# Second branch of the mixer: sums and products on half tiles, products with states ahead of the inner ones, four state buffers

## The reference

```python
def hgrn2_chunked(q, k, v, log_f):
    cum = jnp.cumsum(log_f, axis=-2)
    q_in = q * jnp.exp(cum)
    k_in = k * jnp.exp(-cum)
    intra = jnp.where(causal, jnp.einsum('bhnid,bhnjd->bhnij', q_in, k_in), 0.0)
    last = cum[..., -1:, :]
    k_dec = k * jnp.exp(last - cum)
    chunk_decay = jnp.exp(last[..., 0, :])

    def step(state, xs):
        qi, ki, vi, ai, di = xs
        o = jnp.einsum('bhcd,bhde->bhce', qi, state) + jnp.einsum('bhij,bhje->bhie', ai, vi)
        state = di[..., :, None] * state + jnp.einsum('bhcd,bhce->bhde', ki, vi)
        return state, o
```

## Time and profile before

| | us |
|---|---|
| timed runs, median of 3 | 2370.7 |
| lowest and highest of them | 2370.43 and 2371.64 |
| span of the profiled execution | 2370.3 |
| stretch of the inner matrices, until the loop starts | 7.4 |
| stretch of the loop over the four tiles | 39.6 |

### The profile page before, as it was taken

One profiled execution on the slowest core, in us unless ns is written; L12 is line 12 of the kernel. 1 busy time (PEld: TensorE's weight loads), 2 busy tenths in 40 slices (PEclk: granted clock), 3 DMA queues, 4 the chain that ended last, 5 costly groups with the idle time before them and its releaser, 6 DMA issues. The chain is left out here.

```text
span 2370.3 us, 29415 instructions
## 1 busy us (share of the span) xinstructions
PE 2262.8 (95%) x11234; PEld 1794.2 (76%) x11234; DVE 1506.0 (64%) x1871; ACT 1269.6 (54%) x1680; POOL 276.4 (12%) x273
## 2 busy tenths in 40 slices
PE   7999999999999999999999999999995999999994
PEld 6878558777777768998888878888774777777773
DVE  3534842569978677656334555355337899988886
ACT  4334541588874436552324423235424888888884
POOL 2000000123320212330000000000001111121210
PEclk9999999999999999999999999999996999999997
DMA  6222103423214433001222212334125999999995
GB/s 232 72 71 89 36 21 112 131 76 100 97 61 139 155 125 125 2 1 54 89 95 94 96 36 81 124 115 160 54 101 227 376 408 409 409 402 401 400 401 193
DMA packets 119817, 377.41 MB, mean 159 GB/s; under 512 B 9608, under 2 KB 38592, under 8 KB 94496
## 3 DMA queue, kind: packets, MB, share of 16 engines
q1 hardware_dynamic: 106432, 332.49, 38.0%
q0 software_dynamic: 12768, 37.13, 4.7%
q10 hardware_dynamic: 512, 6.34, 0.6%
HBM read 363.02 MB, written 21.02 MB: 162 GB/s over the span
## 5 line engine op out<-in xcount | busy, mean ns | idle before, releaser
L2270 DVE TENSOR_TENSOR w_lo<-raw,w_hi 128x2048 fp32r<-128x2048 f32 x117 | 267.9, 2290 | 460.0 <-ACT w_hi L1618 459.7
L1618 ACT ACTIVATE w_hi<-raw 128x2048 fp32r<-128x2048 f32 x117 | 223.8, 1913 | 407.5 <-PE bank L863 368.6
L863 PE MATMUL bank<-hT_hi,w_hi 128*128 128x512 f32 x512 | 201.6, 394 | 4.6 <-DVE hT_lo L2334 2.3
L863 PE MATMUL bank<-hT_hi,w_lo 128*128 128x512 f32 x512 | 200.6, 392 | 0.0
L863 PE MATMUL bank<-hT_lo,w_hi 128*128 128x512 f32 x512 | 200.5, 392 | 0.0
L1072 PE MATMUL bank<-hT_hi,w_hi 128*128 128x512 f32 x432 | 173.8, 402 | 0.9 <-DVE hT_lo L2334 0.9
L1072 PE MATMUL bank<-hT_hi,w_lo 128*128 128x512 f32 x432 | 168.2, 389 | 0.0
L1072 PE MATMUL bank<-hT_lo,w_hi 128*128 128x512 f32 x432 | 168.1, 389 | 0.0
L3106 DVE TENSOR_TENSOR e_lo<-eraw,e_hi 128x2048 fp32r<-128x2048 f32 x62 | 141.9, 2290 | 36.1 <-ACT e_hi L2150 36.0
L2990 DVE TENSOR_TENSOR e_lo<-raw,e_hi 128x2048 fp32r<-128x2048 f32 x64 | 146.6, 2291 | 8.2 <-ACT e_hi L2133 7.9
L2990 DVE TENSOR_TENSOR w_lo<-raw,w_hi 128x2048 fp32r<-128x2048 f32 x64 | 144.2, 2286 | 8.9 <-ACT w_hi L2133 8.8
(11 more groups left out here) (590 smaller groups left out, 5344.0 us busy)
## 6 DMA issues: line engine op xcount, KB each, us to landing
raw<-expert_w_gate SPq DMA_DIRECT2D x64, 1024.0 KB, 11.1
raw<-expert_w_up SPq DMA_DIRECT2D x64, 1024.0 KB, 11.6
eraw<-expert_w_down SPq DMA_DIRECT2D x64, 1024.0 KB, 10.8
raw<-w_in SPq DMA_DIRECT2D x40, 1024.0 KB, 5.1
raw<-even_w_in SPq DMA_DIRECT2D x18, 1024.0 KB, 5.3
raw<-odd_w_in SPq DMA_DIRECT2D x16, 1024.0 KB, 5.4
raw<-even_w_out SPq DMA_DIRECT2D x8, 1024.0 KB, 5.1
raw<-odd_w_out SPq DMA_DIRECT2D x8, 1024.0 KB, 5.1
```

What stands on the lines that cost most here:

```text
L863: mm = pe.matmul(out, st, mv, start=first and x == 0, stop=last and x == 2)
L1618: act.activation(split_to(m)[0][:], raw[n % RAW][:], ACT.Copy).then_inc(sem("hi_done"), 1)
L2270: dve.tensor_tensor(split_to(m)[1][:], raw[split_of[m] % RAW][:], f32(split_to(m)[0][:]), ALU.subtract).then_inc(sem("lo_done"), 1)
```

## The change

The inner matrices are made for the two halves apart: for every head and tile two products of a 128 x 64 stationary operand with 64 moving columns, one into partitions 0 to 63 and one into 64 to 127, both into the same 64 columns of the bank. The masked result `hwithin` has 64 columns for each head and tile in place of 128, and the mask is stored accordingly.

The chunk sums of a tile go through the two groups of four heads, and in each head the half s = 0 is followed at once by s = 1. For the last tile only s = 0 is summed. The products with states stand together for the eight heads (`from_states`), and behind them all inner products (`from_chunks`), each of these now two products of 64 rows and 64 columns. The state ahead of the first chunk, which is zero, is neither cleared nor multiplied; the first state is a copy of the first sum. There are four state buffers, and a new semaphore `hs_read` tells DVE that PE has read the states of a tile. The last state isn't formed. The barrier of PE behind the loop is replaced with waits for the last state and for the last output copied.

```diff
+HF = P // 2
+UP, LOW = slice(0, HF), slice(HF, P)
+HALVES = (UP, LOW)
+    in_half = lambda m: m[:, :HF] | m[:, HF:]
-        (i <= j) & same(QC),
+        np.concatenate([in_half((i <= j) & same(QC))] * 2, 1),
+    hwithin = view("hwithin", 0, [P, NT, HEADS, HF], at=8192)
-    hstate = [view(f"hstate{b}", 5, [P, HEADS, P], at=4096 * b) for b in range(3)]
+    hstate = [view(f"hstate{b}", 5, [P, HEADS, P], at=4096 * b) for b in range(4)]
...
             for t in range(NT):
-                ts = slice(t * P, t * P + P)
-                mm = pe.matmul(psum[h][:, ts], hexp[:, h, ts], hqT[:, h, ts], start=True, stop=True)
+                for r in HALVES:
+                    ts = slice(t * P + r.start, t * P + r.stop)
+                    mm = pe.matmul(psum[h][r, t * HF:t * HF + HF], hexp[:, h, ts], hqT[:, h, ts], start=True, stop=True)
...
+        def chunk_sums(t):
+            chunks = range(2 if t < NT - 1 else 1)
+            for hg in range(2):
+                if t:
+                    pe.wait_ge(*after("hs_S", HEADS * (2 * t - 1) + 4 * hg + 4))
+                else:
+                    pe.wait_ge(*after("h_mask", 2 + hg + 1))
+                for h in range(4 * hg, 4 * hg + 4):
+                    for s in chunks:
+                        mm = pe.matmul(psum[2 * s + hg][:, (h % 4) * P:(h % 4) * P + P], hkd[HALVES[s], h, t],
+                                       hv[HALVES[s], t, h * P:h * P + P], start=True, stop=True)
+                        if h % 4 == 3:
+                            mm.then_inc(sem("hs_kv"), 1)
+        def out_bank(t, h):
+            return psum[4 + 2 * (t % 2) + h // 4], slice((h % 4) * P, (h % 4) * P + P)
+        def from_states(t):
+            for h in range(HEADS):
+                bk, cs = out_bank(t, h)
+                if h % 4 == 0 and t >= 2:
+                    pe.wait_ge(*after("hs_o", 2 * (t - 2) + h // 4 + 1))
                 pe.wait_ge(*after("hs_S", HEADS * 2 * t + h + 1))
+                for s, r in enumerate(HALVES):
+                    if t or s:
+                        mm = pe.matmul(bk[r, cs], hqT[:, h, t * P + s * QC:t * P + s * QC + QC], hstate[(2 * t + s) % 4][:, h],
+                                       start=h % 4 == 0, stop=False, skip_group_check=True)
+            mm.then_inc(sem("hs_read"), 1)
+        def from_chunks(t):
+            for h in range(HEADS):
+                bk, cs = out_bank(t, h)
+                for s, r in enumerate(HALVES):
+                    mm = pe.matmul(bk[r, cs], hwithin[r, t, h], hv[r, t, h * P:h * P + P], start=t == 0 and s == 0 and h % 4 == 0,
+                                   stop=True, skip_group_check=True)
+                if h % 4 == 3:
+                    mm.then_inc(sem("hs_ope"), 1)
-        stage()
+        chunk_sums(0)
+        pe.wait_ge(*after("h_mask", HEADS))
+        for t in range(NT):
+            from_states(t)
+            from_chunks(t)
+            if t < NT - 1:
+                chunk_sums(t + 1)
+        stage(wait=False)
+        pe.wait_ge(*after("hs_S", HEADS * (2 * NT - 1)))
+        pe.wait_ge(*after("hs_o", 2 * NT))
 ...
-            dve.tensor_tensor(hintra[:, :, h], psum[h][:].rearrange("p (t j) -> p t j", j=P),
-                              m_hgrn.unsqueeze(1).to_broadcast([P, NT, P]), ALU.mult).then_inc(sem("h_mask"), 1)
+            dve.tensor_tensor(hwithin[:, :, h], psum[h][:, 0:NT * HF].rearrange("p (t j) -> p t j", j=HF),
+                              m_hgrn[:, 0:HF].unsqueeze(1).to_broadcast([P, NT, HF]), ALU.mult).then_inc(sem("h_mask"), 1)
-        own.link(dve.memset(hstate[0][:], 0.0))
-            for s in range(2):
+            for s in range(2 if t < NT - 1 else 1):
-                s_in, s_out = hstate[n % 3], hstate[(n + 1) % 3]
+                s_in, s_out = hstate[n % 4], hstate[(n + 1) % 4]
-                        dve.wait_ge(*after("hs_kv", 2 * n + h // 4 + 1))
+                        dve.wait_ge(*after("hs_kv", 4 * t + (2 if t < NT - 1 else 1) * (h // 4) + s + 1))
-                        if n >= 2:
-                            dve.wait_ge(*after("hs_ope", 2 * ((n - 2) // 2) + 2))
+                        if n >= 3:
+                            dve.wait_ge(sem("hs_read"), (n - 3) // 2 + 1)
+                    if n:
+                        dve.scalar_tensor_tensor(s_out[:, h], s_in[:, h], col(DEC8 + 8 * h + n), kv, ALU.mult, ALU.add).then_inc(sem("hs_S"), 1)
+                    else:
+                        dve.tensor_copy(s_out[:, h], kv).then_inc(sem("hs_S"), 1)
```

More of the change, by code:

```diff
@@ L1376, in _ @@
                 pe.wait_ge(*after("hs_S", HEADS * 2 * t + h + 1))
-                for s in range(2):
-                    r = slice(s * QC, s * QC + QC)
-                    pe.matmul(bk[r, cs], hqT[:, h, t * P + s * QC:t * P + s * QC + QC], hstate[(2 * t + s) % 3][:, h],
-                              start=True, stop=False, skip_group_check=True)
-                mm = pe.matmul(bk[:, cs], hintra[:, t, h], hv[:, t, h * P:h * P + P], start=False, stop=True,
-                               skip_group_check=True)
+                for s, r in enumerate(HALVES):
[9 more added lines that the diff above has]
+                                   stop=True, skip_group_check=True)
                 if h % 4 == 3:
                     mm.then_inc(sem("hs_ope"), 1)
-        stage()
+        chunk_sums(0)
[8 more added lines that the diff above has]
+        pe.wait_ge(*after("hs_o", 2 * NT))
         gemm(pn["og_b"], hT, False)
@@ L2922, in _ @@
             dve.wait_ge(*after("h_in", h + 1))
-            dve.tensor_tensor(hintra[:, :, h], psum[h][:].rearrange("p (t j) -> p t j", j=P),
-                              m_hgrn.unsqueeze(1).to_broadcast([P, NT, P]), ALU.mult).then_inc(sem("h_mask"), 1)
+            dve.tensor_tensor(hwithin[:, :, h], psum[h][:, 0:NT * HF].rearrange("p (t j) -> p t j", j=HF),
+                              m_hgrn[:, 0:HF].unsqueeze(1).to_broadcast([P, NT, HF]), ALU.mult).then_inc(sem("h_mask"), 1)
         stage()
-        own.link(dve.memset(hstate[0][:], 0.0))
         for t in range(NT):
-            for s in range(2):
+            for s in range(2 if t < NT - 1 else 1):
                 n = 2 * t + s
-                s_in, s_out = hstate[n % 3], hstate[(n + 1) % 3]
+                s_in, s_out = hstate[n % 4], hstate[(n + 1) % 4]
                 for h in H8:
                     if h % 4 == 0:
-                        dve.wait_ge(*after("hs_kv", 2 * n + h // 4 + 1))
+                        dve.wait_ge(*after("hs_kv", 4 * t + (2 if t < NT - 1 else 1) * (h // 4) + s + 1))
                         if n:
                             dve.wait_ge(*after("hs_S", HEADS * n))
-                        if n >= 2:
-                            dve.wait_ge(*after("hs_ope", 2 * ((n - 2) // 2) + 2))
+                        if n >= 3:
+                            dve.wait_ge(sem("hs_read"), (n - 3) // 2 + 1)
                     kv = psum[2 * s + h // 4][:, (h % 4) * P:(h % 4) * P + P]
-                    dve.scalar_tensor_tensor(s_out[:, h], s_in[:, h], col(DEC8 + 8 * h + n), kv, ALU.mult, ALU.add).then_inc(sem("hs_S"), 1)
+                    if n:
+                        dve.scalar_tensor_tensor(s_out[:, h], s_in[:, h], col(DEC8 + 8 * h + n), kv, ALU.mult, ALU.add).then_inc(sem("hs_S"), 1)
+                    else:
+                        dve.tensor_copy(s_out[:, h], kv).then_inc(sem("hs_S"), 1)
         stage()
```

16 lines of the change are left out of this document (removed).

## The result

| | us |
|---|---|
| changed kernel, median of 4 | 2349.75 (2349.20 to 2355.68) |
| kernel before, beside it, median of 4 | 2370.56 (2370.35 to 2371.64) |
| ratio | 0.9915, 95% interval 0.9903 to 0.9927 |
| span of the profiled execution | 2347.7; its own time 2349.93 |

The kernel is faster by 20.8 us, or 0.85%.

What follows compares the result with a forecast made beforehand. PE was taken as the bound; loop -15.4, inner matrices -1.7 and loop end -0.2 summed to -17.3 us, span 2353.0, forecast 2353.4 us. The 8-in-10 range was 2350.5 to 2361; the forecast's own, 2350.5 to 2356.5.

Steps and rivals of the forecast that it cites:

- What bounds the kernel: Whole kernel and changed stretch: PE sets the pace ahead of, in and behind the change, so the gain carries through.
- Sums, states, inner products: Loop tile: 16 side-by-side steps per group, 1.79, 1.71 and 1.71 us, plus 0.54 for three shape changes; 5.75 us.
- The 0.1 us a tile added for DVE: Loop: DVE's state updates and PE's arrival nearly level, so each tile was allowed 0.1 us more, 5.85.
- The inner matrices: Ahead of the loop: 128 half-size records take 5.6 us with the shape change, against 7.2; -1.7 us, ends 0 and -3.6.
- the lower bound: Inner matrices: halves fully side by side, 64 steps of 0.053 us, 3.4 us, or 3.6 with the shape change.
- the middle between two ends: Inner matrices: 5.4 us taken between 6.8 one after another and 3.4 side by side, doubting PE's record start rate.
- The end: Behind the loop: PE waits for ACT's last copy, no longer for its 0.19 us mark; -0.2 us.
- The cleared state: Loop start: dropping the first state's clearing and copies gains nothing, as the sums of s = 1 hide them.
- Fourth buffer and last state: Loop: fourth state buffer and `hs_read` cost nothing; the states dropped at the end were included in the loop's -15.4 us.
- The inner products don't run side by side: Rival, loop: halves writing one bank go one after another, 6.8 us more, 2360.2 us; chance 0.20.
- No pair lasts: Rival, loop and inner matrices: side-by-side pairs occur only in bursts; no change, 2371.3 us; chance 0.07.
- The clock falls: Rival, stretch: granted clock drops to 1.2 GHz, steps double, gemm behind loses about 2 us; 2378.8 us; chance 0.05.

Runs made afterwards that it cites:

- experiment 8: Changed kernel with 84 needless 512-column products put ahead of the first products with states, restoring the old timing behind them: 2372.02 us, ratio 1.0005.
- experiment 10: Changed kernel with the output gate's gemm begun early and the chunk sums also cut by key columns into 64 x 64 quadrants: 2353.53 us, stretch 29.82.
- Experiment 9: Changed kernel with the output gate's gemm started on its first two banks before the last two output copies: 2351.86 us, stretch 0.81 us less.
- experiment 2: Kernel before with only the chunk sums reordered, both halves of a head following each other: 2365.78 us, stretch 5.14 us less.
- experiment 6: Changed kernel with the cleared first state and its products put back: 2350.36 us, stretch 0.56 us more.
- experiment 3: Kernel before with only the states' products of all heads placed ahead of the inner products, still 128 wide: 2361.08 us, stretch 9.68 us less.
- experiment 1: Kernel before, unedited, timed and profiled again: 2371.44 us, ratio 1.0001.
- experiment 4: Kernel before with only the inner matrices and their products cut into 64-wide halves, old order: 2364.45 us, stretch 4.94 us less.

## Why the prediction was right, and where it was not

**What bounds the kernel**: right. The stretch's gain reached the end, as far as experiment 8 can tell, and no engine took PE's place.

**Sums, states, inner products**: right in mechanism and size. Forecast for a tile were 1.97, 1.89 and 1.89 us, each with its change of shape; measured 1.98, 1.90 and 1.90. The 0.1 us a tile added for DVE wasn't needed: PE finds the states ready. With it gone the loop is 23.16 us (1373.48 to 1396.64) and not 23.6, -15.8 in place of -15.4.

**The inner matrices**: the term that was mis-sized, and the cause of nearly all that the sum lacks. They run side by side, near the lower bound: 3.88 us for the 64 steps and a change of shape, where the bound had 3.6. The first sums of before started here:

```profile
1379.41 3.50 PE L1364 MATMUL bank<-hv,hkd 64*128 64x128 f32 x32
```

So from the first transpose to the first sum it was 1379.41 - 1368.62 = 10.79 us and is 1373.48 - 1365.95 = 7.53 now: **-3.3 us, forecast -1.7**. The step that failed was the middle between two ends for fear of a limit on how fast PE starts records. At this rate no such limit shows: 128 loads and 128 products begin within 3.9 us, one every 15 ns, and experiment 10 was no slower, with 64 loads done in 1.74 us where the inner matrices' 128 took 3.81. What makes a step 0.060 us (3.81 for 64 pairs of loads) and not 0.053 is open. The two ends were not equally likely by the rows: the only row of halves that share rows and differ in columns, L1379, showed them side by side.

Here the measurement stands against the rule of the Trainium skill (TensorE: Matmul & The Clock Gate, Packing small matmuls) that a load overlaps only where the row group differs: these halves have all rows in common, and their 128 loads are done in 3.81 us beside the products.

**The end**: forecast -0.2, measured -0.03: from the last inner product's end to the gemm it is 0.74 us where it was 0.77. PE no longer waits for ACT's mark, but it still waits for the copy ahead of it. Its start stands 0.09 us behind the copy's end (1397.29, then 1397.38), and stood 0.14 behind it before (1419.02, then 1419.16). The mark begins before the copy has ended, so it never held PE up by its 0.19 us of length. Experiment 9 shows what the wait itself costs: 0.81 us.

**The cleared state**: priced at nothing, worth 0.56 us (experiments 2 and 6). The reason given, that the sums of s = 1 hide it, was true of the order before and falls with the change itself. The forecast of the loop was made from scratch without the clearing, so the sum doesn't suffer; whoever had made the change without that part would have missed 0.56 us. Fourth buffer and last state: nothing, as forecast.

**Sum.** -3.3 - 15.8 and nothing at the end make -19.1, against -17.3. The parts that were measured apart make nearly the same: 9.68 for the states ahead (experiment 3), 5.14 for the sums (2), 0.56 for the cleared state (6), 3.3 for the inner matrices and 0.08 a tile for the inner products are 19.0. From 2370.7 the -19.1 leads to 2351.6, which is inside the stated range, and the pooled executions have 2351.7; that the two agree to 0.1 us is partly luck, since neither is known to that. So the mis-sized terms alone would not have put the result outside. What did is the second step that failed, the allowance for scatter: the remaining 1.9 us down to the first median of 2349.75 are mostly scatter between executions, since three of those four lay at the low end of the fourteen. How much of them is the dip of experiment 8, up to 1.5 us, stays open. I had read the three timed runs of before, 1.2 us wide, as the scatter of the kernel, and set the low end of the range with 0.6 us for it. Fourteen executions spread over 6.5 us. I also had the profiled execution 0.4 us under the median; its time is some 2 us above its span (2349.93 for 2347.7), so, if the kernel before adds as much (experiment 1: 2372.91 for 2371.0), it was itself a slower one, near 2372. It has a dip of the clock near 20 us that experiment 1 lacks, and one near 660 that the changed kernel's first profile lacks.

**Rivals.** *The inner products don't run side by side*: refuted. 32 records of different rows go to one bank in 1.96 us. The Trainium skill (TensorEngine Tiling (Array Packing), Gotcha 1) says that different row tiles cannot access one bank at the same time, and leaves the order to software. Nothing takes turns in this trace, where the two halves lie in different partitions of the bank. What the prediction sets against that from the Trainium skill (PSUM — Partial Sum Buffer, PSUM bank collisions raise a hardware error) was measured there on pairs of different engines, so it doesn't bear on two products of PE. *No pair lasts*: refuted by experiments 2 and 4. *The clock falls*: it is 1.00 in the whole stretch. It does fall elsewhere, in both versions. No run shows the 2 us that this rival puts on the gemm behind the loop; the dip of experiment 8 went with 1.5 us.

What is not settled: why the clock dips near 20, 660 and 1615 us in some executions and not in others. The pause of PE ahead of each is there in both cases and nearly as long, so the rows give no cause; and for the third it is open whether the change itself spares the kernel the dip.

## What to carry to other kernels

Price a sequence of small products by three counts: steps of the slower of two halves side by side, one change of stationary shape (0.18 to 0.19 us here) for every place where the shape changes, and the cover that a shortened step used to give to its neighbours. Group products of one shape across the heads before making them smaller: the order alone gave 9.7 us of 19.1. Where an edit has a stretch of its own, compare the stretch in two profiles, which repeats to 0.01 us, and let the medians, which scatter by several, confirm only the sum. Then compare the rest of the two profiles at fixed marks as well: a shift in time can spare or bring a dip of the clock far behind the edit, which a run with the gain put back undoes along with it.

## What the runs showed of the hardware

- Halves that share all rows and differ in columns (128 x 64 stationary, 64 moving) run side by side for 64 pairs on end: 3.95 us for 128 float32 records, one pair every 60 ns or so.
- Halves that share neither rows nor columns run side by side into one bank: 32 records of 128 moving columns in 1.96 us.
- Four quadrants at a time are sustained too: 64 records in 1.98 us.
- Where the stationary shape changes, PEld stands idle: 0.17 us at most changes, with 4 records ahead of it as with 32, but 0.12 from sums to states' products and 0.07 from inner matrices to sums. A group of 16 steps with its change takes 1.90 us, 0.19 more than 16 steps of 0.107.
- With one and the same program, the granted clock dipped in some stretches in one execution and not in the next, behind pauses of PE of about 2 us that were there both times. Behind a pause of 1.8 us one such dip went with 1.5 us of later work (364.6 against 363.1 us to the router).
- The time outside of the changed stretch ranged from 2316.2 to 2322.8 us over the profiles of this study.
